# An MoE block behind an attention block in one program: 23 weight slots in place of 20, the order of SP's transfers, and the router's chain

## What is computed

```python
h = rms_norm(x, mix_norm_g)
proj = h @ w_in                 # pool, q and kv latents, k_rope, xq, gate logits
y_pool = pool_mixer(...)        # trailing means, then 4 small matrices
y_mla = causal attention, 8 heads of 128 + 64, from the latents (w_uq, w_uk, w_uv)
y_mem = cross attention, 4 heads, over mem (w_mem_kv)
gates = sigmoid(gate_logits + gate_b)          # 3 x 1024
merged = gates[0]*(y_pool @ w_br_pool) + gates[1]*(y_mla @ w_br_mla) + gates[2]*(y_mem @ w_br_mem)
x = x + merged @ w_out
h2 = rms_norm(x, ffn_norm_g)
# router: the best of 4 groups, in it the best 2 of 8 experts, softmax weights
# 32 experts: (silu(xb @ w_gate_e[e]) * (xb @ w_up_e[e])) @ w_down_e[e]
x = rms_norm(x + experts, final_norm_g)
x = second_block(x)             # w_qkv, w_o, w_gate, w_up, w_down
```

## Time and profile before

| | us |
|---|---|
| three runs | 834.97 (median), 834.58, 836.5 |
| the profiled execution | 836.61 |
| its span, first to last instruction | 834.60 |
| PE busy | 760.9 (91%) |
| DVE busy | 405.2 (49%) |
| ACT busy | 326.1 (39%) |
| moved by DMA | 204.58 MB |

### The profile page before, as it was taken

One profiled execution on the slowest core, in us unless ns is written; L12 is line 12 of the kernel. 1 busy time (PEld: TensorE's weight loads), 2 busy tenths in 40 slices (PEclk: granted clock), 3 DMA queues, 4 the chain that ended last, 5 costly groups with the idle time before them and its releaser, 6 DMA issues.

```text
span 834.6 us, 12876 instructions
## 1 busy us (share of the span) xinstructions
PE 760.9 (91%) x5402; PEld 629.2 (75%) x5402; DVE 405.2 (49%) x734; ACT 326.1 (39%) x573; POOL 23.8 (3%) x45
## 2 busy tenths in 40 slices
PE   8989999999999979977768768999998999999996
PEld 8888797888777765544534535999977999999995
DVE  5647755666747451111001004666656655555554
ACT  5466465554443221101001103655566544444442
POOL 1100000000000000000000000300002000000000
PEclk9999999999999979999889879999999999999998
DMA  9636265545793879999999999874432655465301
GB/s 335 211 119 199 78 239 197 196 143 182 286 342 139 328 303 395 421 419 420 422 422 420 422 421 359 302 266 152 141 125 89 203 196 197 163 201 169 134 1 51
DMA packets 83833, 204.58 MB, mean 245 GB/s; under 512 B 6976, under 2 KB 47552, under 8 KB 71232
## 3 DMA queue, kind: packets, MB, share of 16 engines
q1 hardware_dynamic: 83776, 203.75, 65.8%
HBM read 202.69 MB, written 1.05 MB: 244 GB/s over the span
## 4 chain that ended last, share of the span: by engine, by line
PE 71%; DMA 15%; DVE 6%; ACT 3%; SPq 2%; issue 2%; POOL 0%; DVEq 0%; ACTq 0%; POOLq 0%
PE ps L564 53%; PE ps L845 4%; DMA ext<-in_w_gate_e 3%; DMA big<-in_w_up_e 3%; DMA raw<-in_w_up_e 3%; DMA ext<-in_w_up_e 3%; SPq L443 2%; DMA gb<-in_gate_b 2%; PE ps L824 2%; PE ps L866 2%; DVE wl L1420 1%; PE ps L545 1%; PE ps L879 1%; PE ps L926 1%; ACT junk L1078 1%
## 5 line engine op out<-in xcount | busy, mean ns | idle before, releaser
L1420 DVE TENSOR_TENSOR wl<-raw,wh 128x1024 fp32r<-128x1024 f32 (+3 forms) x180 | 213.3, 1200 | 142.3 <-ACT wh L1069 142.0
L1069 ACT CAST wh<-raw 128x1024 fp32r<-128x1024 f32 (+3 forms) x180 | 183.0, 1031 | 103.7 <-PE ps L564 103.5
L564 PE MATMUL ps<-fra,wh 128*128 128x256 f32 x1168 | 215.2, 286 | 6.0 <-DVE fra L1851 2.6
L564 PE MATMUL ps<-wh,fra 128*128 128x512 f32 (+3 forms) x668 | 190.5, 371 | 5.3 <-DVE gb L1644 2.3
L564 PEld LDWEIGHTS ps<-fra,wh 128*128 128x128 f32 x1168 | 185.0, 194 | 8.4 <-DVE fra L1851 2.8
L564 PE MATMUL ps<-fra,wl 128*128 128x256 f32 x584 | 166.6, 285 | 0.0
L564 PEld LDWEIGHTS ps<-wh,fra 128*128 128x128 f32 x668 | 119.4, 190 | 25.8 <-DVE wl L1420 2.7
L564 PE MATMUL ps<-wl,fra 128*128 128x512 f32 (+3 forms) x334 | 121.8, 365 | 0.0
L564 PEld LDWEIGHTS ps<-fra,wl 128*128 128x128 f32 x584 | 113.5, 194 | 0.0
L564 PE MATMUL ps<-wh,frb 128*128 128x512 f32 x240 | 74.4, 391 | 0.0
L564 PEld LDWEIGHTS ps<-wl,fra 128*128 128x128 f32 x334 | 63.3, 190 | 9.8
(11 more groups left out here) (238 smaller groups left out, 740.6 us busy)
## 6 DMA issues: line engine op xcount, KB each, us to landing
ext<-in_w_up_e SPq DMA_DIRECT2D x18, 1024.0 KB, 26.1
raw<-in_w_in SPq DMA_DIRECT2D x16, 1024.0 KB, 5.0
ext<-in_w_gate_e SPq DMA_DIRECT2D x15, 1024.0 KB, 26.0
raw<-in_w_down_e SPq DMA_DIRECT2D x14, 1024.0 KB, 22.6
ext<-in_w_down_e SPq DMA_DIRECT2D x13, 1024.0 KB, 26.5
raw<-in_w_qkv SPq DMA_DIRECT2D x12, 1024.0 KB, 12.5
raw<-in_w_gate_e SPq DMA_DIRECT2D x11, 1024.0 KB, 27.2
raw<-in_w_gate SPq DMA_DIRECT2D x11, 1024.0 KB, 5.1
```

Source lines behind the costliest of these rows:

```text
L564: t = e.matmul(o, a, w, start=first and n == 0, stop=final and n == 2, skip_group_check=not check)
L1069: e.copy(halves(q)[0], piece_view(q)).then_inc(*up("wh", q))
L1420: e.tensor_tensor(l, piece_view(q), h.bitcast(F), ALU.subtract).then_inc(*up("wl", q))
```

## The change

- `RAW` 7 to 8 and `BIG` 3 to 4: one more slot in `raw`, a fourth in `big` (1792 to 3840, free when the router's logits are done), and one made of `gb` (free when the gains of the norm are used). 23 slots. To make room, XE, CM and sel have one buffer each (`hot` and `weighed` for sel), the constants and `rt` are smaller, and the causal mask is read as two overlapping slices of one.
- The order of `ring` is new, and so is that of SP's list: expert matrices 0 to 8 are issued one at a time, each behind a dense unit (`expert_at`), and some of them with a wait of their own, ahead of all that follows in the list. The bias rows stand at other places (`bias_at`). The final gains (`gfin`) are loaded after the last group's up products.
- Router: both second-half residual additions and both copies of transposes now stand ahead of the last product with the gains on DVE; PE has twelve idle products (`warm(WARM[4], 1)`) between the logits and the ranks; the count of tokens per expert stands behind the first group's products.
- DVE writes the weighed matrix of a group after the product of silu and up, no longer with the hot one.

The diff, cut to its core:

```diff
-RAW = 7
+RAW = 8
-BIG = 3
+BIG = 4
-WARM = (24, 16, 12, 9)
+WARM = (24, 16, 12, 9, 12)
@@ Weights.plan
-        self.early = ([(self.slot[u], u) for u in apart] + [(RAW + EXT + z, None) for z in range(BIG)]
-                      + [(RAW + z, None) for z in (8, 9, 6, 7)])
         left = [(self.slot[u], u) for u in freed[-DENSE:]]
-        ring = self.early + left + [(RAW + z, None) for z in (4, 5, 0, 1, 2, 3)]
+        near, far = ([(RAW + z, None) for z in (h, 2 + h)] for h in (self.half_first, 1 - self.half_first))
+        ring = ([(RAW - 1, None)] + [(self.slot[u], u) for u in apart] + [(RAW + EXT + z, None) for z in (1, 2, 3)]
+                + [(RAW + z, None) for z in (8, 9)] + left[:1] + [(RAW + z, None) for z in (6, 7)] + left[1:]
+                + near + [(RAW + z, None) for z in (4, 5)] + far + [(RAW + EXT, None), (RAW + EXT + BIG, None)])
@@ program
-    XE = [big[:, 1024 * z:1024 * z + 1024].rearrange("p (t n) -> p t n", t=8) for z in range(2)]
-    CM = [big[:, 2048 + 256 * z:2304 + 256 * z] for z in range(2)]
-    sel = [big[:, 2560 + 512 * z:3072 + 512 * z] for z in range(2)]
+    XE = big[:, 0:1024].rearrange("p (t n) -> p t n", t=8)
+    CM = big[:, 1024:1280]
+    hot, weighed = big[:, 1280:1536], big[:, 1536:1792]
@@ sync
-        bias_at = {first_unit("gate", br, c) + DENSE + 1: n for n, (br, c) in enumerate(branches)}
-        early = wt.dense_end
+        def expert(n):
+            if n == 3:
+                e.wait_ge(*at("values", "m", 7))
+            if n == 6:
+                e.wait_ge(*at("piece", last["br", 2, 1]))
+            if n == 9:
+                e.wait_ge(*at("piece", last["br", 1, 1]))
+            if n == 15:
+                e.wait_ge(*at("piece", wt.half_use))
+            if n == 17:
+                e.wait_ge(*at("piece", last["out", 1]))
+            if n == 21:
+                e.wait_ge(*at("logits", 1))
+            if n == 22:
+                e.wait_ge(*at("h2 rest"))
+            fetch(wt.dense_end + n)
+        bias_at = {first_unit(*key) + k: n for n, (key, k) in enumerate((
+            (("gate", 2, 0), 0), (("gate", 2, 1), 0), (("gate", 1, 0), 0), (("gate", 1, 1), 1), (("br", 1, 0), 1),
+            (("br", 1, 1), 1)))}
+        expert_at = {first_unit(*key) + k: n for n, (key, k) in enumerate((
+            (("uv", 0), 0), (("gate", 2, 0), 0), (("gate", 2, 0), 1), (("gate", 2, 1), 1), (("br", 2, 1), 0),
+            (("gate", 1, 0), 1), (("br", 1, 1), 0), (("br", 1, 1), 1), (("out", 1), 1)))}
         for u in range(DENSE, wt.dense_end):
             if u in bias_at:
                 gate_bias(bias_at[u])
             fetch(u)
-            if bias_at.get(u) in (0, 4):
-                for _ in range(2 if bias_at[u] == 0 else BIG):
-                    fetch(early)
-                    early += 1
...
+            if u in expert_at:
+                expert(expert_at[u])
...
-        load("pm", gb[:, 0, :], grow[2:3, :].to_broadcast([P, 1024]))
+        for n in range(RAW):
+            if n == 5:
+                e.wait_ge(*at("taken", "eu", 7))
+                load("gfin", gb[:, 1, :], grow[1:2, :].to_broadcast([P, 1024]))
+                load("pm", gb[:, 0, :], grow[2:3, :].to_broadcast([P, 1024]))
+            fetch(wt.expert_end + n)
@@ tensor
             logits(4, i)
+        warm(WARM[4], 1)
         enter(0, "ranked")
...
         gather(0)
-        count()
         for g in range(8):
...
             experts(g)
+            if g == 0:
+                count()
@@ vector
         whole(out1)
-        first_residual(1, 0)
+        for i in range(2):
+            first_residual(1, i)
+        for i in range(2):
+            turned_residual(4, i)
         e.wait_ge(*own())
         gains(1, 0)
-        first_residual(1, 1)
-        for i in range(2):
-            turned_residual(4, i)
```

More of the change, by code:

```diff
@@ L361, in program @@
     wg_, wu_, wd_ = raw[:, 0, :], raw[:, 1, :], raw[:, 2, :]
+    wide_slots = [big[:, 1792 + 2048 * z:3840 + 2048 * z] for z in range(BIG)]
     def slot_view(u):
@@ L382, in piece_view @@
         return slot_view(p.unit)[:, p.first:p.first + p.rows, :]
-    s_slot = [sem(f"s_slot{z}") for z in range(RAW + EXT + BIG)]
+    s_slot = [sem(f"s_slot{z}") for z in range(RAW + EXT + BIG + 1)]
     def landed(u):
@@ L479, in sync @@
             fetch(u)
-            if bias_at.get(u) in (0, 4):
-                for _ in range(2 if bias_at[u] == 0 else BIG):
-                    fetch(early)
-                    early += 1
-            if u == first_unit("gate", 1, 1) + DENSE:
-                e.wait_ge(*at("piece", last["br", 2, 1]))
-                for _ in range(2):
-                    fetch(early)
-                    early += 1
-        assert all(u < wt.dense_end for u in bias_at), bias_at
-        e.wait_ge(*at("piece", last["br", 1, 1]))
-        for u in range(early, wt.expert_end):
-            n = u - wt.dense_end
-            if n == len(wt.early):
+            if u in expert_at:
+                expert(expert_at[u])
+        for n in range(9, wt.expert_end - wt.dense_end):
+            if n == 9:
                 e.wait_ge(*at("merged", 5, 1))
                 load("gffn", gb[:, 0, :], grow[0:1, :].to_broadcast([P, 1024]))
-                load("gfin", gb[:, 1, :], grow[1:2, :].to_broadcast([P, 1024]))
-            if n == len(wt.early) + DENSE:
-                e.wait_ge(*at("piece", last["out", 1]))
-            fetch(u)
+            expert(n)
         e.wait_ge(*at("counted"))
@@ L824, in gather @@
                         t = e.matmul(bank[2 + a][:, P * (kk % 4):P * (kk % 4) + P], H[:, i, P * kk:P * kk + P],
-                                     sel[z][:, P * i:P * i + P], start=(i == 0), stop=(i == 1))
+                                     hot[:, P * i:P * i + P], start=(i == 0), stop=(i == 1))
                 t.then_inc(*up("gathered", g, a))
@@ L831, in gather_weights @@
             for i in range(2):
-                t = e.transpose(bank[1][:, P * i:P * i + P], sel[g % 2][:, 256 + P * i:384 + P * i], ident)
+                t = e.transpose(bank[1][:, P * i:P * i + P], weighed[:, P * i:P * i + P], ident)
             t.then_inc(*up("CM turned", g))
@@ L878, in combine @@
                         enter(b, "MO", i, c)
-                    t = e.matmul(bank[b][:, :], CM[g % 2][:, P * i:P * i + P], YE[c], start=(g == 0), stop=(g == 7))
+                    t = e.matmul(bank[b][:, :], CM[:, P * i:P * i + P], YE[c], start=(g == 0), stop=(g == 7))
                     if g == 7:
@@ L1802, in gather @@
             e.wait_ge(*at("gathered", g, 1))
-            e.tensor_copy(XE[g % 2][:, 4:8, :], bank[3][:, :].rearrange("p (j n) -> p j n", j=4)).then_inc(*up("XE dve", g))
+            e.tensor_copy(XE[:, 4:8, :], bank[3][:, :].rearrange("p (j n) -> p j n", j=4)).then_inc(*up("XE dve", g))
         select(0)
+        weigh()
+        select_weights(0)
         gather(0)
-        e.wait_ge(*at("count"))
-        e.tensor_reduce(tm_[:, 0, :], bank[6][:, 64:96], AX, ALU.max).then_inc(*routed())
-        e.wait_ge(*own())
-        e.tensor_copy(flag[:, :], tm_[:, 0, :]).then_inc(*up("counted"))
         for g in range(8):
@@ L1817, in vector @@
                 select(g + 1)
+            if g == 0:
+                e.wait_ge(*at("count"))
+                e.tensor_reduce(tm_[:, 0, :], bank[6][:, 64:96], AX, ALU.max).then_inc(*routed())
+                e.wait_ge(*own())
+                e.tensor_copy(flag[:, :], tm_[:, 0, :]).then_inc(*up("counted"))
             e.wait_ge(*at("expert silu", g))
@@ L1820, in vector @@
             if g < 7:
+                select_weights(g + 1)
                 gather(g + 1)
```

47 lines of the change are left out of this document (24 added, 23 removed).

## The result

The changed kernel takes 839.84 us (median of 9 runs, 837.95 to 841.42) where the kernel before took 834.97 in the same comparison. The ratio is 1.0047, 95% interval 1.0033 to 1.0061: 3.9 us longer by the ratio (2.8 to 5.1), 4.9 by the medians. 834.1 was forecast, so the direction was wrong, though the time lies in the range.

What follows compares the result with a forecast made beforehand. The bound was the full DMA stretch of expert matrices, begun by the first slot reuse, then TensorE. Terms put that reuse +6.6 us later, slots gave -7.5: -0.9 us in all, 834.1 us against 834.97, range 830.5 to 840.0.

Steps and rivals of the forecast that it cites:

- The stall of the values-head-7 wait: After the causal attention: TensorE waits for the third bias row, +12.2 us, then runs at half clock, +2.0 us.
- The units that sit behind the wait are not late themselves.: SP's list behind the wait for head 7: w_br_mem lands near 206 us, before its use, so no further cost.
- The last bias row in front: Sixth bias row, near 250 us: with one matrix ahead instead of five, TensorE's pauses and half clock shrink, -4.2 us.
- The router: Second residual addition no longer waits for a gains product of 1.16 us; most comes back, leaving -0.2 us.
- the count: The token count's two products leave the path ahead of the first expert group, -0.3 us.
- Twelve idle products: Between the router's logits and the ranks: they keep TensorE's clock up through ranks and first gather, -2.9 us.
- rival A: Router: the clock is not kept up despite the idle products, so the time is about 838 us; chance 0.27.
- Three more slots: Expert weights: 23 slots in place of 20 shorten the full DMA stretch by 2.52 us each, -7.5 us.
- Rival C: Expert weights: one of the three added slots brings nothing, the rest as forecast, 836.6 us; chance 0.08.
- I take all behind 518.96 us as unchanged.: The part behind the experts, where TensorE is the bound, keeps its time: no change.

Runs made afterwards that it cites:

- Experiments 3 and 4: Two variants of the changed kernel: the first without the twelve idle products, ratio 1.0072; the second with 21 weight slots in place of 23, ratio 1.0101.
- Experiment 1: The changed kernel with the third bias row moved ahead of expert matrix 3 and its wait for head 7's values: 833.37 us, ratio 0.9975.
- experiment 8: The kernel before with the sixth bias row moved ahead of the five expert matrices it stood behind: 831.60 us, ratio 0.9961.
- experiment 12: The kernel before with twelve idle products added between the router's logits and the ranks: 832.11 us, ratio 0.9962.
- experiments 13 and 14: Changed kernel with wait further down, gating first, four more idle products and rel_ext first; then SP's program padded (ratio 0.9835) or VectorE's instead (0.9822).

## Why the prediction was wrong

By D, the second profile of the changed kernel (without the spells near 265 and 313) stands 9.2 us above the kernel before (160.75 against 151.51), where I had 6.6. The last "up" matrix follows the reuse in 176.71 instead of 184.23 us: 7.5 us less, where I had 7.5. What comes behind it is 1.7 us longer, where I had nothing. That makes +3.4 in place of -0.9; the ratio says +3.9. Step by step:

- **The stall of the values-head-7 wait, +12.2 and +2.0.** The place, the queue ahead of the row and the length were right (12.60 and 12.86). The half clock (1.2 GHz) cost 2.0 us in the first profile (3.9 us at half), as I had it, and 3.05 in the second (6.1 us). Experiments 3 and 4 have the same stop (12.64 and 12.95 us) and lose 1.6 and 1.5 behind it, so the mean of the four is 2.0. Taking the wait out of the way brought 16.0 us by D and 15.8 by the ratios, and I had 14.2. Of the 1.8 by which D differs, about 0.7 is the length of the stop and 1.0 the long spell of the second profile, from which D is taken.
- **"The units that sit behind the wait are not late themselves."** It held only because the first stop hid it. Experiment 1 shows what was underneath: with the third row in time, the fourth costs a stop of 6.5 us and a spell at half clock. Moving the row alone takes away less than half of the price, where my account of the stall suggests all of it.
- **The last bias row in front, -4.2.** This is a term that was too large: 3.3 by D and by the ratio of experiment 8. I left 0.4 us for the wait for VectorE's gating, and 1.6 stayed, behind which four of eight profiles lost another 1.7 at half clock.
- **The router, -0.2, and the count, -0.3.** Not measured alone. What the other terms leave of D is 151.5 - 3.3 - 2.6 - 144.7 = 0.9 us, if they add up, where I had 0.5.
- **Twelve idle products, -2.9.** Right: 2.6 by D and 3.2 by the ratio in the kernel before. The clock was kept through the gather in twelve of thirteen profiles, so rival A is not what happened; the first profile of the changed kernel, with 5.29 us, is the thirteenth. Pauses of 0.9 and 0.76 us lost the clock in four profiles of eight. The rule that I weighed in the prediction (the Trainium skill, "TensorE: Matmul & The Clock Gate", section "Why this matters for your kernels") asks only that no gap between bursts be over some 3 us. These pauses are far shorter and the clock fell all the same; the measurement decides.
- **Three more slots, -7.5.** Right in the traces (7.5), and 2.5 us a slot in experiment 4. Rival C is out.
- **"I take all behind 518.96 us as unchanged."** This step failed: a term put at nothing measured 1.7 us. 0.6 us came in before the long run of products (155.99 us behind the last "up" matrix, 155.42 before, both with a spell at half clock there). I took it for rel_ext, which lands behind later loads of gains and stands on the chain of the first profile, though not of the second. The runs show rel_ext's price, 1.0 to 1.3 us, only where the clock is kept there: 155.93 and 156.20 us with it behind, 154.69 with it first, 154.94 in the kernel before (experiment 12). Where the clock falls, variants of one order differ by 0.3 to 0.4 us. 1.1 us came in behind the start of the long run, from a fetch of VectorE's instructions beside the last output (experiments 13 and 14).

Terms with opposite signs of 14 and 15 us made a forecast of -0.9. The misses are 1.8 for the stop, 0.9 for the row, 0.3 for the idle products, 1.7 behind the experts and 0.4 the other way in the router: 4.3 us, from -0.9 to +3.4. No single one of them turns the sign: without the largest the sum would still be +1.6. What failed is the list of terms as a whole, each off by up to 2 us where their sum was forecast at less than one, and most of all two of them: the stretch taken as unchanged, and the last bias row, of whose pauses half stayed. The medians are 4.9 apart, since of the two clusters that either kernel's times fall into the median before sits in the lower and the median after in the upper; the ratio's 3.9 is the fairer number.

What stays open: what the 0.6 us at the start of the second block are in these two profiles, which may be chance (experiment 8, the kernel before with one row moved, has 155.67); why the same program loses the clock in the same short pause in one execution and not in the next, and how the remaining 0.9 us divide between the new order of the residuals and the count.

## What to carry to other kernels

In a list that one queue works off in order, a wait is paid for by everything behind it, so the place for a wait on something late is behind all that is needed earlier; moving one victim ahead of it only uncovers the next. Price it by going down the list and noting for each transfer when it is needed, and count the burst that forms behind the wait as a cost of its own. Where large terms cancel, the sum is no better known than its largest terms. Measure between two points inside the program, so that luck ahead of them drops out, and don't assume that a part without edits keeps its time: here a changed VectorE program moved a fetch of instructions beside the last output.

## What the runs showed of the hardware

- A fetch of 8 KB of VectorE's instructions beside a 256 KB output transfer made it land after 3.28 us instead of 2.13, in all profiles of the changed kernel and its variants but one: with sixty more writes in VectorE's program (experiment 14) the fetch was gone from there and the transfer took 2.13 us.
- With much queued, SP takes longer to issue: 4.43 us for the sixth of seven 1 MB transfers in a row, 0.34 for the first (experiment 1). A quarter MB issued behind them took 14.2 us to land, where it took 3.27 us on an idle queue.
- The granted clock went to half after two pauses of 0.9 and 0.76 us in four of eight profiles of the same instructions. After a stop of 12.6 to 12.95 us it stayed at half for 3.9 us of products in one profile and 6.1 in another of the same program, and for 3.2 and 3.0 in two variants (experiments 3 and 4).
